# A low-rank operand laid out twice so that neighbouring products use different row groups, and the last norm's vector applied ahead of its root

## The reference, cut to what matters

```
xw = p[..., 3 * C:3 * C + W_LORA]              # 32 columns
xa = p[..., 3 * C + W_LORA:3 * C + W_LORA + A_LORA]   # 32 columns
w = -jax.nn.softplus(-(w0 + jnp.tanh(xw) @ w_up)) - 0.5      # w_up 32 x 512
a = jax.nn.sigmoid(a0 + xa @ a_up)                           # a_up 32 x 512
...
h = h + 0.5 * swiglu(n, ffn2_w_gate[l], ffn2_w_up[l], ffn2_w_down[l])
return rms_norm_2(h, final_norm)[:, N_META:]   # h * rsqrt(mean(h * h) + eps) * final_norm
```

## Time and profile before

| what | us |
|---|---|
| median of 3 runs | 963.79 (962.06 to 966.03) |
| the profiled execution, its own time | 964.37 |
| its span | 962.5 |
| TensorE matmul busy | 920.7 (96%) |
| ScalarE, VectorE, GpSimd busy | 536.2, 466.1, 639.9 |
| granted clock over the span | 0.991 of full speed |

### The profile page before, as it was taken

The page is one execution under the profiler, slowest core; times in us unless marked ns, Lnnn a source line. Parts: engine busy times, 40 slices in busy tenths (PEclk is TensorE's granted clock), DMA queues, the critical chain, the costliest instruction groups (busy, mean ns, idle before and its releaser), DMA issues.

```text
span 962.5 us, 24183 instructions
## 1 busy us (share of the span) xinstructions
PE 920.7 (96%) x9532; PEld 878.1 (91%) x9532; DVE 466.1 (48%) x862; ACT 536.2 (56%) x793; POOL 639.9 (66%) x277
## 2 busy tenths in 40 slices
PE   9999999999998899999999999999878999999996
PEld 8988778999997689999999989999768999999996
DVE  5348544767799673333321143772546633333112
ACT  6677675666757584444444356675533664444431
POOL 3797344677997077877777755653532688888882
PEclk9999999999999999999999999999999999999999
DMA  7665324345534144555555534422001455555551
GB/s 271 232 201 181 113 79 141 110 154 176 176 122 150 40 151 158 196 173 173 172 173 177 174 111 140 147 95 86 4 26 68 154 177 195 174 191 194 184 175 44
DMA packets 41246, 140.98 MB, mean 146 GB/s; under 512 B 4548, under 2 KB 7492, under 8 KB 41160
## 3 DMA queue, kind: packets, MB, share of 16 engines
q1 hardware_dynamic: 39392, 138.28, 43.1%
q10 hardware_dynamic: 1768, 1.46, 0.6%
HBM read 138.66 MB, written 1.06 MB: 145 GB/s over the span
## 4 chain that ended last, share of the span: by engine, by line
PE 61%; DVE 9%; issue 8%; POOL 4%; ACT 2%; POOLq 0%; DVEq 0%; ACTq 0%
PE ps L836 60%; POOL wlo L747 4%; DVE wlo L2232 2%; DVE hA L2695 1%; DVE qkl L2232 1%; ACT ps L1656 1%; DVE ivt L2241 1%; DVE mad L2464 1%; DVE ps L2232 1%; DVE hT L2270 0%; DVE mixT L2241 0%; DVE hA L2683 0%; DVE aL L2241 0%; ACT whi L1736 0%; DVE ps L2241 0%
## 5 line engine op out<-in xcount | busy, mean ns | idle before, releaser
L747 POOL TENSOR_TENSOR wlo<-ring,whi 128x1024 fp32r<-128x1024 f32 x244 | 587.7, 2424 | 276.4 <-ACT whi L1736 267.8
L1736 ACT ACTIVATE whi<-ring 128x1024 fp32r<-128x1024 f32 x251 | 264.4, 1060 | 197.0 <-PE ps L836 178.5
L836 PE MATMUL ps<-aH,whi 128*128 128x272 f32 (+1 forms) x1032 | 301.6, 292 | 3.3 <-DVE ps L2241 1.4
L836 PE MATMUL ps<-aH,wlo 128*128 128x272 f32 (+1 forms) x1032 | 295.9, 287 | 0.0
L836 PE MATMUL ps<-aL,whi 128*128 128x272 f32 (+1 forms) x1032 | 295.3, 286 | 0.0
L836 PEld LDWEIGHTS ps<-aH,whi 128*128 128x128 f32 x1032 | 195.9, 190 | 8.3 <-issue 5.3
L836 PEld LDWEIGHTS ps<-aL,whi 128*128 128x128 f32 x1032 | 195.8, 190 | 0.6 <-issue 0.5
L836 PEld LDWEIGHTS ps<-aH,wlo 128*128 128x128 f32 x1032 | 196.0, 190 | 0.0
L836 PE MATMUL ps<-fxH,whi 128*128 128x256 f32 x480 | 135.7, 283 | 4.6 <-DVE fxL L2232 2.0
L836 PE MATMUL ps<-fxL,whi 128*128 128x256 f32 x480 | 135.0, 281 | 0.0
L836 PE MATMUL ps<-fxH,wlo 128*128 128x256 f32 x480 | 134.9, 281 | 0.0
(11 more groups left out here) (389 smaller groups left out, 1339.3 us busy)
## 6 DMA issues: line engine op xcount, KB each, us to landing
ring<-in_stream SPq DMA_DIRECT2D x253, 512.0 KB, 3.3
xT<-in_x SPq DMA_DIRECT2D x4, 272.0 KB, 3.7
out<-hT SPq DMA_DIRECT2D x4, 256.0 KB, 2.6
row<-in_row SPq DMA_DIRECT2D x1, 768.0 KB, 6.0
cst<-in_cst SPq DMA_DIRECT2D x1, 621.0 KB, 4.7
cst<-in_cst SPq DMA_DIRECT2D x1, 576.0 KB, 4.5
mem<-gate_rows_d ACTq DMA_DIRECT2D x1, 512.0 KB, 6.7
mat<-in_mat SPq DMA_DIRECT2D x1, 512.0 KB, 4.3
```

The costliest lines, as they stand in the source:

```text
L747: nc.gpsimd.tensor_tensor(wlo[:, s, :], ring[:, s, :], whi[:, s, :].bitcast(F32), ALU.subtract).then_inc(S("w_split"), 1)
L836: return nc.tensor.matmul(out, lhsT, rhs, start=start, stop=stop, skip_group_check=True)
L1736: nc.scalar.activation(whi[:, v % SLOTS, :], ring[:, v % SLOTS, :], ACT.Copy).then_inc(S("w_high"), 1)
```

## The change

The 64 low-rank columns of unit 0 are laid out as 128: xw, xw, xa, xa. The mixing vectors follow, and the up-projections lie four times in mat (w_up on rows 0 to 31 and 32 to 63, a_up on rows 64 to 95 and 96 to 127). The tanh covers 64 rows. The four products of a set take their rows in turn from the one copy and the other.

At the end ScalarE multiplies each tile of xT by the vector ahead of the root (weighted_tile): tiles 0 to 5 into PSUM banks 4, 5 and 6, tiles 6 and 7 into hT. Tiles 0, 1 and 4 follow their own square; tiles 2 and 3 wait until the running sum has left bank 5, and are made behind the square of tile 5 together with tile 5. When rstd is there, VectorE makes three products of two tiles each from PSUM (last_norm) and GpSimd one of the two tiles in hT. SyncE issues the transfers of tiles 0 to 5 as VectorE goes on, and that of tiles 6 and 7 last. The filler of the last norm goes to bank 7.

```diff
+    LORA_ROWS = np.concatenate([r(3072, 3104)] * 2 + [r(3104, 3136)] * 2)
...
-            unit(w_in[:, 3072:3136] if P_RWKV[j] == 12 else w_in[:, 3136:3232])
+            unit(w_in[:, LORA_ROWS] if P_RWKV[j] == 12 else w_in[:, 3136:3232])
...
-    vec[:64, VEC["mu"] + 12] = mu[1536:1600]
+    vec[:, VEC["mu"] + 12] = mu[LORA_ROWS - 1536]
...
-    mat[0:32, MAT["wup"]:MAT["wup"] + 512] = f["rwkv_w_up_2"][0]
-    mat[32:64, MAT["wup"]:MAT["wup"] + 512] = f["rwkv_a_up_2"][0]
+    for at, up in ((0, "w"), (32, "w"), (64, "a"), (96, "a")):
+        mat[at:at + 32, MAT["wup"]:MAT["wup"] + 512] = f[f"rwkv_{up}_up_2"][0]
...
+        def last_tile(k):
+            return hT[:, k, TM:TT] if k >= 6 else ps[:, (4, 5, 6)[k // 2], (k % 2) * T:(k % 2 + 1) * T]
...  SyncE
-                sp.wait_ge(S("norm_h"), (len(NORMS) - 1) * KT + k + 2)
+                if k < 6:
+                    sp.wait_ge(S("last_out"), k // 2 + 1)
+                else:
+                    sp.wait_ge(S("last_out_b"), 1)
...  GpSimd
+            pool.wait_ge(S("last_x"), KT)
+            pool.wait_ge(S("norm_rstd"), len(NORMS))
+            nc.gpsimd.tensor_tensor(hT[:, 6:, TM:TT], hT[:, 6:, TM:TT], mid(rstd[:, 0:T], 2), ALU.mult).then_inc(S("last_out_b"), 1)
...  TensorE
-            def filler(n):
+            def filler(n, b=6):
-                    mm(ps[:, 6, 0:432], C("ones"), cst[:, 0:432])
+                    mm(ps[:, b, 0:432], C("ones"), cst[:, 0:432])
-                    filler(1)
+                    filler(1, 7 if tag == "final" else 6)
...
+            def low_rank(row0, sem):
+                for j in range(4):
+                    rows = slice(row0 + 32 * (j % 2), row0 + 32 * (j % 2) + 32)
+                    m = mm(ps[:, 4 + j, 0:TT], mat[rows, MAT["wup"] + j * P:MAT["wup"] + (j + 1) * P], pr[rows, 12, 1:1 + TT])
+                m.then_inc(S(sem), 1)
             def decay_rates():
                 pe.wait_ge(*once("lora_th"))
-                for j in range(4):
-                    m = mm(ps[:, 4 + j, 0:TT], mat[0:32, MAT["wup"] + j * P:MAT["wup"] + (j + 1) * P], pr[0:32, 12, 1:1 + TT])
-                m.then_inc(S("lora_w"), 1)
+                low_rank(0, "lora_w")
             def learning_rates():
                 pe.wait_ge(*once("decay_th"))
-                for j in range(4):
-                    m = mm(ps[:, 4 + j, 0:TT], mat[32:64, MAT["wup"] + j * P:MAT["wup"] + (j + 1) * P], pr[32:64, 12, 1:1 + TT])
-                m.then_inc(S("lora_a"), 1)
+                low_rank(64, "lora_a")
...  ScalarE
+            def weighted_tile(k):
+                if k == 2:
+                    act.wait_ge(S("norm_sum"), sums_up_to("final"))
+                func(last_tile(k), xT[:, k, TM:TT], ACT.Identity, "last_x", scale=V("final", k))
...
                         square(tag, k, c0, n)
+                        if tag == "final":
+                            for i in {2: (), 3: (), 5: (2, 3, 5)}.get(k, (k,)):
+                                weighted_tile(i)
...
-                    func(pr[0:32, 12, 1:1 + TT], pr[0:32, 12, 1:1 + TT], ACT.Tanh, "lora_th")
+                    func(pr[0:64, 12, 1:1 + TT], pr[0:64, 12, 1:1 + TT], ACT.Tanh, "lora_th")
...  VectorE
+            def last_norm():
+                r = rstd[:, 0:T]
+                dve.wait_ge(S("norm_rstd"), len(NORMS))
+                for k in range(0, 6, 2):
+                    dve.wait_ge(S("last_x"), 6)
+                    nc.vector.tensor_tensor(hT[:, k:k + 2, TM:TT], ps[:, (4, 5, 6)[k // 2], :].rearrange("p (a t) -> p a t", a=2),
+                                            mid(r, 2), ALU.mult).then_inc(S("last_out"), 1)
...
-            norm("final", TM, T, "final")
+            last_norm()
```

## The result

The changed kernel took 958.99 us, the median of its runs, against 962.06 for the kernel before in the same measurement (the ratio is 0.9945, 95% interval 0.9926 to 0.9964, which is 3.5 to 7.1 us on 962). The medians are 3.1 us apart. One of the changed kernel's five runs was a slow one, 1468.35 us at a granted clock of 0.556: the ratio leaves it out, and without it the median is 958.66. Measured twice more, on two chips, each time beside the kernel before, the changed kernel took 959.59 against 963.49 (ratio 0.9967, 0.9956 to 0.9978) and 960.49 against 963.20 (0.9971, 0.9957 to 0.9985). Over the three, the medians are 2.7 to 3.9 us apart. I had said 961.4, with a range of 959.7 to 963.3; 958.99 is outside.

A forecast was written before the change was run, and what follows sets the result against it. The prediction took TensorE, busy for 96% of the span, to bound the kernel, and the transfers to nearly limit the output. From 964.37 it took 1.84 (sets), 0.75 (clock) and 0.35 (end): 961.4 us, range 959.7 to 963.3.

The forecast's parts named there:

- part 2: Behind the first low-rank set, the clock's fall goes: 0 to 1.5 us, taken as 0.75.
- Part 1: Mixer's two low-rank sets: products on alternating row groups overlap, 0.92 us less per set, 1.84 for both.
- The rival that they don't overlap: Low-rank sets: products don't overlap at 32 rows, only the end gains: 964.0 us, or 963.4 from the median; chance 0.08.
- Part 3: Output end: transfers limit it, so mainly the earlier first issue counts; 0 to 0.8 us, taken as 0.35.
- The clock falls anyway: Near 580 the clock still drops behind the shorter sets, or earlier runs mostly lacked the fall: 962.2 us; chance 0.15.
- The end is worth more: Output end: four transfers in flight bring the whole 0.8 us; with the whole clock term 960.2 us; chance 0.08.
- The clock falls elsewhere: Mixer's recurrence behind 690: falls come to lie otherwise; two more make it slower, 964.6 us; chance 0.05.

The follow-up runs named there:

- the end alone: The kernel before with only the new end of the change and the old mixer: 963.11 us against 963.49, ratio 0.9995.
- laid out twice: The changed kernel, but each set takes all four products from one copy, so nothing alternates: 962.94 us against 963.07 for the kernel before, ratio 1.0001.
- the 32-row set of twice the products: The kernel before with the pause filled and each first-set product made twice on the same 32 rows: 965.77 us against 963.20, ratio 1.0005.
- The products made twice: The changed kernel with each pair of low-rank products made twice, in both sets: 961.09 us against 963.07 for the kernel before, ratio 0.9977.
- the kernel with the pause filled: The kernel before with one 208-column product on all rows ahead of its wait for the tanh: 960.78 us against 963.07, ratio 0.9971.

## Why the prediction was wrong

**Two terms of the sum were mis-sized: where it starts, and the clock of part 2.** The larger is the start. The sum begins at 964.37, the profiled execution's own time. The prediction saw that this lay 0.58 above the median of before, 963.79, and put no term for it. In the measurement beside the changed kernel the median of before was 962.06, which is 2.3 us below the start, nearly the whole 2.4 us between 961.4 and 958.99. In the later measurements it was 963.49, 963.07 and 963.20, 0.9 to 1.3 us below the start.

The second is the clock term. Its size was known: 15 matmuls at 0.10 us each, 1.5 us, measured as 7.74 - 6.25 = 1.49. I took half of it, 0.75, because the runs of before spread by 4 us and I read into that spread that some of them did not have this fall. The traces taken don't bear this out. In all four traces of a first set that kept its 32-row order, its 2.03 us and its pause (before, before again, the end alone, laid out twice) the fall is there. In the eight with a short set, a paired set or a filled pause ahead of 2.03 us it isn't. The only other trace with a fall there is that of the 32-row set of twice the products. The spread has other places as well, the HGRN stage and the recurrence.

With the whole clock term the sum is 960.7 from the profiled execution, and with the 3.5 us that the traces show, 960.0 from the median of 963.5 that before had in a later measurement; the changed kernel had 958.99, 959.59 and 960.49. The reduction that I forecast, 964.37 - 961.4 = 2.9 us, is close to the 3.1 between the medians of the first measurement. That is luck: the traces show 3.5, and the medians of the other two differ by 3.9 and 2.7.

**The reason for the clock's part was right only in part.** The fall went, as said. I argued from length: 1.50 us of pause and 32-row work would be harmless, as the second set's 2.03 was. The products made twice show that length isn't what decides by itself: 0.39 + 2.03 us in pairs keep the clock up. No run has a short set that isn't paired, so whether the shorter time alone would have been enough stays open.

**The range was too narrow below.** The median of before moved too: 963.79 in its first runs, 962.06 when they were continued beside the changed kernel. My range took in the unknown costs and not what a median of a few runs does when the HGRN stage and the mixer's recurrence each add or lose 1 us by chance. A range down to 958.5 would have said so.

**Part 1 was right.** 0.91 and 0.92 us for the two sets, against 0.92 each. 32-row neighbours overlap just as the 64-row rows of the attention had shown, and nothing behind TensorE was late: the windows behind the first set have it busy throughout. The rival that they don't overlap is refuted by the timeline, and the laid-out-twice kernel shows that no other part of the change carries it.

**Part 3 was right in its limit, a little high in its size.** VectorE's three products take 0.7 us each to complete and 1.89 together, GpSimd's 1.27, done at 952.87, before VectorE's third at 953.43, with no sign that the two hold each other up. The last issue comes earlier too, and the end gained 0.2 us, not 0.35: only the first issue counted, at the same 94% of the DMA engines. I had added 0.17 for fewer gaps between the transfers; there were none to close. ScalarE's last multiplication took 0.51 us instead of 0.42, and was done 0.50 us ahead of the root (950.03, to 950.53), as said.

**The rivals.** "The clock falls anyway" did not happen. "The end is worth more" is refuted (0.2 of 0.8). "The clock falls elsewhere" is half true: the mixer's recurrence between 690 and 740 does change its falls from run to run, but not only in the changed kernel. The windows of 720 to 740 in the kernel laid out twice, whose mixer has the timing of before, and of 690 to 720 and 720 to 740 in the kernel with the pause filled:

```profile
720.00:740.00 20.00, 16.42 (x269) 15.41 (x269) 8.56 (x19) 4.51 (x10) 3.74 (x2) 0.74 0.24 82
```

```profile
690.00:720.00 30.00, 25.22 (x995) 23.26 (x997) 13.07 (x24) 10.33 (x22) 11.61 (x10) 0.94 0.12 40
720.00:740.00 20.00, 17.75 (x237) 16.49 (x230) 13.66 (x28) 8.95 (x17) 3.68 (x2) 1.00 0.16 54
```

Granted clocks of 0.74 and 1.00 in a stretch that had 0.91 in the earlier trace rows, and 0.83 in the second trace of the kernel before. In the kernel with the pause filled the fall isn't gone but lies earlier: 690 to 720 has 0.94, where the kernel before has 1.00. Whether the earlier start of the recurrence makes it faster on average stays open. From the second set's end to the root the two traces of the kernel before have 366.5 and 366.7 us, the three of the changed kernel 365.9, 365.0 and 367.0, so the 0.65 of the table is less than what traces of one kernel differ by.

## What to carry to other kernels

Short products on few rows can cost twice, their own time and the clock of the full-size work behind them. Here pairing them on different row groups took away both costs, and a filler product in the pause directly ahead of them took away the second. Where the DMA engines are over 90% busy once the output transfers run, bringing the first issue forward shortens the end, and only by a part if it takes one more transfer (0.1 us of 0.27 here). Start the sum from a median of many runs, not from the profiled execution. When a fall of the clock has a cause in the trace of before that the change removes, count it whole, and take a second trace of the kernel before to see whether it is chance.

## What the runs showed that I had not expected

- One fp32 product of 208 columns on all rows, put into a pause of 0.39 us, made the kernel 2.3 us faster by the medians (ratio 0.9971, 0.9958 to 0.9983), of which the trace shows 1.49 behind the set. That is much of what the whole change brought.
- The same 0.39 us of pause and 2.03 us of low-rank work bring the fall with 32 rows at a time and don't with pairs on 64.
- The two 32-row products of a pair start some 7 ns apart, and a pair costs what one does: eight records in 1.19 us, sixteen in 2.10.
- Removing the filler ahead of the last sums opened a pause of 0.27 us and still gained 0.19.
